# First loads in pieces with zero products, the query statistic moved into the attention steps, and twelve low parts moved from GpSimd to VectorE

## The chip, the core and the metric

The kernel runs on one core of one Trainium2 chip. The metric is the device time of one execution in microseconds. Engines are called TensorE (PE in the profile), VectorE (DVE), ScalarE (ACT), GpSimd (POOL) and SyncE (SP).

## What is computed

Four layers act on a stream of 272 tokens (16 meta tokens and 256 others) of width 1024, in fp32. Only what the change touches is shown; the rest is MLPs, a short convolution, a spatial gating mixer and convolutional feed-forward layers, all of them products with weight matrices of 1024 to 4096 rows.

```python
hn = rms_norm(h, g_mix[0])
z = hn @ w_in                                   # c_q, c_kv, k_pe, fox q, fox k, fox v, forget logit
q = (rms_norm(c_q, g_cq) @ w_uq).reshape(b, l, 8, 96)
q = rope_tail(rms_norm(q, g_q_mla), cos, sin)   # one statistic for each token and head
o_fox = blocked_causal_attention(qf, kf, vf, 64 ** -0.5, cum_log_f)   # 8 "fox" heads
o_mla = blocked_causal_attention(q, k, v_mla, 96 ** -0.5)             # 8 MLA heads
...
g, xb = jnp.split(h @ w_in, 2, axis=-1)         # recurrent mixer, width 1536
bterm = mult * (i * xb)
_, hs = lax.associative_scan(_lin_rec_op, (a, bterm), axis=1)
y = (hs * gelu(g)) @ w_out
```

## The kernel before

Activations lie feature-major: 128 features on the partitions, tokens along the free dimension. A weight matrix is cut into blocks of 128x128, and eight blocks (six in the down projections) make a unit. A product is done in three parts with both operands split into a high part (rounded) and a low part (the rest): high x high, high x low of the activation, low of the weight x high. So a unit of eight blocks is 24 matmuls on TensorE, into one PSUM bank. ScalarE makes the high part of each unit of weights (`split_hi`, L338), VectorE the low part (`split_lo`, L343), three units ahead (`LA = 3`), from slabs of two units (1024 KB) that SyncE loads into four places (`raw`). The same split is made of each activation: ScalarE makes `xhi` (L459), GpSimd `xlo` (L468), after VectorE has multiplied by the gain (`xg`, L449).

The order of the work is written out by hand for each engine; engines meet only at semaphores, and each runs its own list in order.

**The start.** ScalarE issues the load of the stream `h` (1088 KB), then the constants and selection rows; SyncE issues `params`, then the slabs. VectorE multiplies by the gain into two alternating buffers, so a third waits for GpSimd's low part of the first. TensorE waits for the constants, then does unit 0, waiting at each block for its `xlo`, then unit 1, then the column sum of `ssum` (`pe_stats`, L422), for which VectorE has added up eight squares (L1159). ScalarE takes the root (L435), VectorE the inverse (`rstd`, L442). Output tiles go round four PSUM banks: unit 4 starts when tile 0 has been read, which on VectorE needs `rstd` (L1231, L1232). Then come the forget gate (L1265 to L1278, on ScalarE L1590) and the statistic of the fox queries, whose inverse goes to TensorE at L852.

**The query statistic.** After the query projections (L956 to L958) TensorE does `q_stats` (L895): 42 small matmuls of 8 columns, in three groups. ScalarE takes the root (`roots(3)`, L1515, L1517), VectorE inverts and scales it (L1294 to L1304), and only then do the softmax steps begin, though the values are needed from item 9 on (the MLA heads). The attention goes over 18 items: item 0 and item 9 are small ones for the meta tokens, items 1 to 8 the fox heads, 10 to 17 the MLA heads. At step `st` TensorE does `scores(st)` (L995, L997), now and then a `spread` (L852), `turn(st - 2)`, the transposes of the probabilities (L1017, L1019), and `values(st - 3)` (L1033 to L1035); VectorE does the peak of the scores (L1313), the normalisation (L1332), a part of the keys up to step 7 (`k_normed`, L1200, L1204), and low parts (L1338); ScalarE the exponential (L1620) and copies.

**The recurrent mixer's end.** Steps `k` of a table (`B_SCAN`, `B_MULT`, `B_HIGH`) place the work. VectorE scans (L1470) and multiplies by the gate (L1475), ScalarE makes the high part (L1764), GpSimd the low part (L1947), for twelve tiles; TensorE's output projection `b_out` starts with two units of six blocks, which need the twelve tiles one after the other. Before it lies a dummy product (L1139).

## Time and profile before

| | |
|---|---|
| median of 3 runs | 1388.16 us (1387.38, 1388.16, 1391.67) |
| the profiled execution, time | 1393.52 us |
| the profiled execution, span | 1391.6 us |
| TensorE busy | 96% of the span |
| VectorE, ScalarE, GpSimd busy | 69%, 53%, 33% |

The span is the time from the first to the last instruction of the profiled execution; its time is 1.9 us longer. TensorE counts as busy while a matmul is in flight, also when the chip has granted it the lower of its two clocks, 1.2 GHz in place of 2.4 GHz; so the share of busy time does not tell of the clock.

### The profile page before, as it was taken

The page shows a single profiled execution, that of the slowest core. Times are in us where ns is not written, and L with a number is a line of the kernel's source. Part 1 is how long each engine was busy: PE and PEld are TensorE (multiplying, and loading weights), DVE is VectorE, ACT ScalarE, POOL GpSimd, SP SyncE. Part 2 cuts the span into 40 slices and gives each one's busy share as a digit, 9 for nine tenths or more (in the row PEclk, how much of TensorE's full clock was granted, in tenths as well). Part 3 has the DMA queues.
Part 4 walks back from the last instruction along what each step waited for, and adds up shares of the span by engine and source line. Part 5 has one row for each costly group of instructions (what it writes and reads, how often), then busy time and mean ns, then how long its engine had stood idle before and what let it go on. Part 6 is the DMA issues. An engine that isn't in the chain of part 4 may idle for free.

```text
span 1391.6 us, 29208 instructions
## 1 busy us (share of the span) xinstructions
PE 1334.9 (96%) x10776; PEld 1298.5 (93%) x10776; DVE 966.0 (69%) x1446; ACT 736.4 (53%) x1224; POOL 462.4 (33%) x492
## 2 busy tenths in 40 slices
PE   5999999999999999999999999999999969999997
PEld 5787699999999999999989999999998859999996
DVE  6767567664477677555655679997578786999844
ACT  5454645444444454444545456665446844766642
POOL 3532044321111443211636324333126563333310
PEclk9998999999999999999999999999999969999998
DMA  7440045555555555555525545554554426455451
GB/s 268 150 149 32 1 152 174 186 185 184 180 181 183 180 180 183 190 187 186 195 92 183 187 175 185 183 182 169 189 202 162 137 94 223 159 191 189 143 203 53
DMA packets 34508, 230.53 MB, mean 166 GB/s; under 512 B 3838, under 2 KB 4990, under 8 KB 10662
## 3 DMA queue, kind: packets, MB, share of 16 engines
q1 hardware_dynamic: 33652, 226.47, 46.8%
q10 hardware_dynamic: 770, 2.90, 0.6%
q8 instruction: 55, 0.90, 0.3%
q14 instruction: 31, 0.25, 0.1%
HBM read 228.17 MB, written 1.05 MB: 165 GB/s over the span
## 4 chain that ended last, share of the span: by engine, by line
PE 77%; issue 8%; DVE 6%; ACT 4%; POOL 4%; DMA 1%; POOLq 0%; DVEq 0%; ACTq 0%; SPq 0%
PE ps L378 25%; PE ps L379 25%; PE ps L380 25%; DVE wlo L343 2%; POOL xlo L468 2%; ACT whi L338 2%; POOL ssum L474 1%; PE ps L1085 1%; DMA raw<-w 1%; DVE rstd L442 1%; DVE work L1470 1%; POOL q_mla L1857 1%; DVE work L1441 0%; PE ps L422 0%; ACT work L1752 0%
## 5 line engine op out<-in xcount | busy, mean ns | idle before, releaser
L343 DVE TENSOR_TENSOR wlo<-raw,whi 128x1024 fp32r<-128x1024 f32 (+1 forms) x448 | 546.5, 1225 | 106.2 <-ACT whi L338 105.2
L378 PE MATMUL ps<-xhi,whi 128*128 128x256 f32 (+2 forms) x2064 | 586.5, 284 | 18.5 <-DVE wlo L343 13.9
L379 PE MATMUL ps<-xlo,whi 128*128 128x256 f32 (+2 forms) x2064 | 584.6, 283 | 0.0
L380 PE MATMUL ps<-xhi,wlo 128*128 128x256 f32 (+2 forms) x2064 | 583.5, 283 | 0.0
L338 ACT ACTIVATE whi<-raw 128x1024 fp32r<-128x1024 f32 (+1 forms) x448 | 448.5, 1008 | 141.2 <-PE ps L380 136.9
L378 PEld LDWEIGHTS ps<-xhi,whi 128*128 128x128 f32 x2064 | 391.9, 190 | 23.2 <-issue 15.9
L380 PEld LDWEIGHTS ps<-xhi,wlo 128*128 128x128 f32 x2064 | 392.3, 190 | 0.0
L379 PEld LDWEIGHTS ps<-xlo,whi 128*128 128x128 f32 x2064 | 389.9, 189 | 0.3
L378 PE MATMUL ps<-hhi,whi 128*128 128x256 f32 (+1 forms) x1184 | 338.0, 285 | 7.7 <-POOL hlo L1947 7.4
L380 PE MATMUL ps<-hhi,wlo 128*128 128x256 f32 (+1 forms) x1184 | 335.7, 283 | 0.0
L379 PE MATMUL ps<-hlo,whi 128*128 128x256 f32 (+1 forms) x1184 | 335.5, 283 | 0.0
L378 PEld LDWEIGHTS ps<-hhi,whi 128*128 128x128 f32 x1184 | 225.9, 191 | 10.6 <-POOL hlo L1947 4.9
L379 PEld LDWEIGHTS ps<-hlo,whi 128*128 128x128 f32 x1184 | 226.2, 191 | 0.0
L380 PEld LDWEIGHTS ps<-hhi,wlo 128*128 128x128 f32 x1184 | 226.1, 191 | 0.0
L468 POOL TENSOR_TENSOR xlo<-xg,xhi 128x256 f32 (+4 forms) x64 | 61.0, 954 | 354.8 <-ACT xhi L459 354.6
L647 POOL TENSOR_TENSOR work<-work 128x256 f32<-128x256 f32 x48 | 66.1, 1376 | 174.6 <-ACT work L603 169.1
L492 DVE TENSOR_TENSOR h<-ps,h 128x256 f32<-128x256 f32 (+3 forms) x64 | 27.2, 424 | 125.1 <-PE ps L380 125.1
L561 POOL TENSOR_TENSOR hlo<-act,hhi 128x258 f32 (+1 forms) x64 | 66.8, 1044 | 117.7 <-ACT hhi L553 117.7
L618 ACT ACTIVATE work<-tmp,params 128x256 f32<-128x256 f32 x96 | 57.7, 601 | 87.0 <-DVE tmp L588 87.0
L459 ACT ACTIVATE xhi<-xg 128x256 fp32r<-128x256 f32 (+4 forms) x64 | 26.6, 420 | 130.9 <-DVE xg L449 130.9
L553 ACT ACTIVATE hhi<-act 128x258 fp32r<-128x258 f32 (+3 forms) x64 | 26.9, 420 | 88.4 <-DVE act L540 88.4
L474 POOL TENSOR_TENSOR ssum<-ssum,sq 128x256 f32<-128x256 f32 (+1 forms) x64 | 45.9, 718 | 58.4 <-ACT sq L455 58.4
(262 smaller groups left out, 1314.3 us busy)
## 6 DMA issues: line engine op xcount, KB each, us to landing
raw<-w SPq DMA_DIRECT2D x184, 1024.0 KB, 4.9
raw<-w SPq DMA_DIRECT2D x40, 768.0 KB, 4.2
h<-x_fm ACTq DMA_DIRECT2D x1, 1088.0 KB, 6.4
out_fm<-h SPq DMA_DIRECT2D x8, 128.0 KB, 2.0
ws<-ws_src ACTq DMA_DIRECT2D x1, 512.0 KB, 5.0
bs<-bs_rows ACTq DMA_DIRECT2D x1, 512.0 KB, 5.8
consts<-constants ACTq DMA_DIRECT2D x1, 508.0 KB, 9.7
q_fox<-decay_rows SPq DMA_DIRECT2D x1, 340.0 KB
```

What stands on the lines that cost most here:

```text
L338: nc.scalar.activation(whi[:, j % HLR, 0:n], raw[:, slot, col:col + n], ACT.Copy).then_inc(whi_done, 1)
L343: nc.vector.tensor_tensor(wlo[:, j % HLR, 0:n], raw[:, slot, col:col + n], whi[:, j % HLR, 0:n].bitcast(F32), ALU.subtract).then_inc(wlo_d ...
L378: nc.tensor.matmul(o, hi, xh, start=start, stop=False)
L379: nc.tensor.matmul(o, hi, xl, start=False, stop=False)
L380: mm = nc.tensor.matmul(o, lo, xh, start=False, stop=stop)
L468: nc.gpsimd.tensor_tensor(xlo[:, kt, c0:c0 + t], xg[:, slot, 0:t], xhi[:, kt, c0:c0 + t].bitcast(F32), ALU.subtract).then_inc(xlo_done, 1)
L474: nc.gpsimd.tensor_tensor(ssum[:, c0:c0 + t], ssum[:, c0:c0 + t], sq[:, slot, 0:t], ALU.add).then_inc(ssum_done, 1)
L492: nc.vector.tensor_tensor(hh, ps[:, jt % ring + (4 - ring), 0:t], hh, ALU.add).then_inc(tile_free, 1)
L553: nc.scalar.activation(hi[:, k, 0:t], src[:, j % 2, 0:t], ACT.Copy).then_inc(uhi_done, 1)
L561: nc.gpsimd.tensor_tensor(lo[:, k, 0:t], src[:, j % 2, 0:t], hi[:, k, 0:t].bitcast(F32), ALU.subtract).then_inc(ulo_done, 1)
L618: nc.scalar.activation(cb[:, j % 4, :], tmp[:, j % 2, 0:SEQ], ACT.Identity, scale=par(f"f_conv_w{layer}", it * (3 * UB) + 3 * j + 2), bias ...
L647: nc.gpsimd.tensor_tensor(half[:, i % 2, :], gg[:, i % 2, :], cb[:, (2 * i + 1) % 4, :], ALU.mult).then_inc(u_done, 1)
```

## The change

Three parts. First, the start: `h` is loaded in four pieces with a semaphore each, `params` in two (the second one behind the slabs and the pad rows), the first slab in two halves; TensorE begins with 18 matmuls on a buffer that VectorE has set to zero, into a bank that is not otherwise in use; four gain buffers take the place of two; VectorE makes the low parts of the odd tiles, GpSimd those of the even ones; unit 0 and unit 1 do all high x high products first, then high x low, then low x high; the column sum goes behind unit 2, the sum of squares to GpSimd alone, and VectorE's inverse, with all that hangs on it, to the place of tile 3. Second, the three groups of `q_stats` go into `turn` of items 2, 3 and 4, into bank 6, `roots(3)` behind ScalarE's step 6, and VectorE's scaling into step 7. Third, the twelve low parts of the recurrent mixer go from GpSimd to VectorE, with a table `B_LOW` one step behind `B_HIGH`, and a step more in the loop.

```diff
-        x_loaded = sem("x_loaded")
+        x_loaded = [sem(f"x_loaded{i}") for i in range(4)]
+        xlo_odd = sem("xlo_odd")
...
-B_STEPS = max(*B_MULT, *B_HIGH, *B_GELU, 31) + 1
+B_LOW = steps(B_R5 + 10, (0, 1), (2, 3), (4, 5), (6, 7), (8, 9, 10, 11))
+B_STEPS = max(*B_LOW, *B_MULT, *B_HIGH, *B_GELU, 31) + 1
...
+        gained = [xg[:, 0, :], xg[:, 1, :], tmp[:, 0, :], tmp[:, 1, :]]
...
-            sp.dma_start(params[:, :], params_in).then_inc(small_in, 16)
+            first = pcol["conv_w"][0]
+            sp.dma_start(params[:, 0:first], params_in[:, 0:first]).then_inc(small_in, 16)
...
+                    half = UB * P
+                    sp.dma_start(raw[:, 0, 0:half], src[0][:, 0:half]).then_inc(s("unit0_loaded"), 16)
+                    sp.dma_start(raw[:, 0, half:cols], src[0][:, half:cols]).then_inc(raw_full[0], 16)
+                    for k in range(1, RAW):
+                        sp.dma_start(raw[:, k, 0:cols], src[k]).then_inc(raw_full[k], 16)
...
+                    rest = pcol["conv_w"][0]
+                    sp.dma_start(params[:, rest:npar], params_in[:, rest:npar]).then_inc(s("params_loaded"), 16)
...
-            pe.wait_ge(consts_in_done, 16)
+            pe.wait_ge(s("warm_set"), 1)
+            for _ in range(WARM):
+                nc.tensor.matmul(ps[:, 7, 0:SEQ], chi[:, 0, 0:P], chi[:, 0, 0:SEQ], start=True, stop=True)
...
+            def q_stats(k):
+
+                if k == 0:
+                    pe.wait_ge(q_eps_step, 6)
+                m = META if k == 2 else P
...
+                    mm = nc.tensor.matmul(ps[0:m, 6, 2 * P + k * HEADS:2 * P + (k + 1) * HEADS], lhs, rhs, start=x < 0,
+                                          stop=x == 5)
+                if k == 2:
+                    mm.then_inc(n_ss, 1)
...
+            def first_unit(u):
+
+                bank = take()
+                o = ps[:, bank, 0:T0]
+                pe.wait_ge(whi_done, u + 1)
+                for b in range(8):
+                    if u == 0:
+                        pe.wait_ge(xhi_done, b + 1)
+                    nc.tensor.matmul(o, whi[:, u, b * P:(b + 1) * P], xhi[:, b, :], start=b == 0, stop=False)
+                for b in range(8):
+                    if u == 0 and b % 2:
+                        pe.wait_ge(xlo_odd, (b + 1) // 2)
+                    elif u == 0:
+                        pe.wait_ge(xlo_done, b + 2)
+                    nc.tensor.matmul(o, whi[:, u, b * P:(b + 1) * P], xlo[:, b, :], start=False, stop=False)
+                pe.wait_ge(wlo_done, u + 1)
+                for b in range(8):
+                    mm = nc.tensor.matmul(o, wlo[:, u, b * P:(b + 1) * P], xhi[:, b, :], start=False, stop=b == 7)
+                mm.then_inc(unit_done, 1)
+
             for u in range(0, U_KN):
-                whole(u)
+                if u < 2:
+                    first_unit(u)
+                else:
+                    whole(u)
+                if u == 2:
+                    pe.wait_ge(consts_in_done, 16)
+                    pe_stats(pe, 0, 0, T0)
...
-            q_stats()
...
+                if j in (2, 3, 4):
+                    q_stats(j - 2)
+                if j == 5:
+                    pe.wait_ge(n_root, 4)
...
-                        pe.wait_ge(n_root, 4)
+                        pe.wait_ge(n_root, 3)
...
+            nc.vector.memset(chi[:, 0, :].bitcast(F32), 0.0).then_inc(s("warm_set"), 1)
             dve.wait_ge(small_in, 16)
-            dve.wait_ge(x_loaded, 16)
-            for kt in range(KT):
-                dve_gain(dve, 0, kt, kt % 2, 0, T0)
-                if kt == 4:
-                    split_lo(dve, 0, 0, 8)
-            for j in range(1, LA):
-                split_lo(dve, 0, j, 8)
-            for kt in range(KT):
-                dve.wait_ge(sq_done, kt + 1)
-                dve.wait_ge(ssum_done, kt + 1)
-                nc.vector.tensor_tensor(ssum[:, :], ssum[:, :], sq[:, kt % 2, :], ALU.add).then_inc(ssum_done, 1)
+
+            def first_gain(kt):
+                dve.wait_ge(x_loaded[kt // 2], 16)
+                if kt >= 4 and kt % 2 == 0:
+                    dve.wait_ge(xlo_done, kt - 2)
+                elif kt >= 4:
+                    dve.wait_ge(xlo_odd, (kt - 3) // 2)
+                nc.vector.tensor_scalar(gained[kt % 4], h[:, kt, :], par(NORM_GAIN[0], kt), None,
+                                        ALU.mult).then_inc(xg_done, 1)
+
+            def first_xlo(kt):
+                dve.wait_ge(xhi_done, kt + 1)
+                nc.vector.tensor_tensor(xlo[:, kt, :], gained[kt % 4], xhi[:, kt, :].bitcast(F32),
+                                        ALU.subtract).then_inc(xlo_odd, 1)
+            for kt in range(4):
+                first_gain(kt)
+            first_xlo(1)
+            first_gain(4)
+            first_gain(5)
+            first_xlo(3)
+            split_lo(dve, 0, 0, 8)
+            first_gain(6)
+            first_gain(7)
+            first_xlo(5)
+            split_lo(dve, 0, 1, 8)
+            first_xlo(7)
             nc.vector.memset(soft[:, :, :, :], 1.0).then_inc(s("soft_set"), 1)
             nc.vector.memset(q_inv[:, :, :], 1.0).then_inc(s("soft_set"), 2)
+            split_lo(dve, 0, 2, 8)
             split_lo(dve, 0, LA, 8)
-            dve_rstd(dve, 0, 0, T0)
...
-                if t == 0:
-
+                if t == 3:
+
+                    dve_rstd(dve, 0, 0, T0)
+                    dve.wait_ge(unit_done, 1)
+                    src = ps[:, 0, 0:T0]
...
-                if t == 1:
+                if t == 3:
...
+            def query_scale():
+                c = q_scale
+                dve.wait_ge(n_root, 4)
...
+                if st == 7:
+                    query_scale()
...
+                for t in B_LOW.get(k, ()):
+                    dve.wait_ge(uhi_done, hid0["b_in"] + t + 1)
+                    nc.vector.tensor_tensor(hlo2[:, t, :], xb[:, t, :], hhi2[:, t, :].bitcast(F32),
+                                            ALU.subtract).then_inc(ulo_done, 1)
...
-            act.dma_start(h[:, :, :], x_in).then_inc(x_loaded, 16)
+            for i in range(4):
+                act.dma_start(h[:, 2 * i:2 * i + 2, :], x_in[:, 2 * i:2 * i + 2, :]).then_inc(x_loaded[i], 16)
             act.dma_start(consts[:, :], consts_in).then_inc(consts_in_done, 16)
             act.dma_start(sel_in, rows_in).then_inc(rows_loaded, 16)
+
+            def first_xhi(kt):
+                act.wait_ge(xg_done, kt + 1)
+                nc.scalar.activation(xhi[:, kt, :], gained[kt % 4], ACT.Copy).then_inc(xhi_done, 1)
             for kt in range(KT):
-                act_xhi(act, 0, kt, kt % 2, 0, T0)
-                if kt in (2, 4, 6):
-                    split_hi(act, 0, kt // 2 - 1, 8, first=True)
+                first_xhi(kt)
+                if kt == 3:
+                    act.wait_ge(s("unit0_loaded"), 16)
+                    nc.scalar.activation(whi[:, 0, :], raw[:, 0, 0:UB * P], ACT.Copy).then_inc(whi_done, 1)
+                if kt in (5, 7):
+                    split_hi(act, 0, (kt - 3) // 2, 8, first=True)
             for kt in range(KT):
                 act_square(act, 0, kt, kt % 2, 0, T0)
-            split_hi(act, 0, LA, 8, first=True)
...
-            act_root(act, 0, 0, T0)
...
+                if t == 2:
+                    act_root(act, 0, 0, T0)
...
-            roots(3)
...
+                if st == 6:
+                    roots(3)
...
+            for kt in range(0, KT, 2):
+                pool.wait_ge(xhi_done, kt + 1)
+                nc.gpsimd.tensor_tensor(xlo[:, kt, :], gained[kt % 4], xhi[:, kt, :].bitcast(F32),
+                                        ALU.subtract).then_inc(xlo_done, 2)
             for kt in range(KT):
-                pool_xlo(pool, 0, kt, kt % 2, 0, T0)
+                pool_ssum(pool, 0, kt, kt % 2, 0, T0)
...
-            for t in range(NB):
-                pool.wait_ge(uhi_done, hid0["b_in"] + t + 1)
-                nc.gpsimd.tensor_tensor(hlo2[:, t, :], xb[:, t, :], hhi2[:, t, :].bitcast(F32),
-                                        ALU.subtract).then_inc(ulo_done, 1)
```

`B_LOW` puts tiles (0, 1) at `B_R5 + 10`, (2, 3) at + 11, (4, 5) at + 12, (6, 7) at + 13 and (8, 9, 10, 11) at + 14; `B_R5` is 21, `B_MULT` begins at + 7 and `B_HIGH` at + 9.

## Rows read from the trace of the kernel before

**Rows 1.** The page: busy time; then the longest waits of TensorE over the span.

```profile
PE 1334.9 (96%) x10776; PEld 1298.5 (93%) x10776; DVE 966.0 (69%) x1446; ACT 736.4 (53%) x1224; POOL 462.4 (33%) x492
...
PE ps L378 <- DVE wlo L343: 13.9, 4, 12.9
PE ps L378 <- POOL hlo L1947: 7.4, 5, 3.6
```

**Rows 2.** Timeline of the start: start us, us, engine line operation.

```profile
7.31 0.63 DVE L449 TENSOR_SCALAR xg<-h,params 128x272 f32<-128x272 f32 x2 [7.31 <-DMA h<-x_fm]
...
9.88 0.43 ACT L459 ACTIVATE xhi<-xg 128x272 fp32r<-128x272 f32 x1 [1.43 <-DVE xg L449]
10.39 0.76 POOL L468 TENSOR_TENSOR xlo<-xg,xhi 128x272 fp32r<-128x272 f32 x1 [0.70 <-ACT xhi L459]
10.47 1.06 ACT L338 ACTIVATE whi<-raw 128x1024 fp32r<-128x1024 f32 x1 [0.15 <-DMA raw<-w]
...
12.89 0.56 PE L378 MATMUL ps<-xhi,whi 128*128 128x272 f32 x1 [12.89 <-DVE wlo L343]
...
23.95 1.22 PE L422 MATMUL ps<-ssum,consts 128*128 128x272 f32 x2 [2.00 <-DVE ssum L1159]
...
24.23 1.28 ACT L435 ACT_TABLE_LOAD   x1
...
25.52 0.49 ACT L435 ACTIVATE root<-ps,params 128x272 f32<-128x272 f32 x1
...
26.04 1.85 DVE L442 RECIPROCAL rstd<-root 128x272 f32<-128x272 f32 x1 [0.57 <-ACT root L435]
```

**Rows 3.** DMA from 3 to 5 us: packets and MB of SyncE's queue (q1) and ScalarE's (q10).

```profile
q10 hardware_dynamic: 69, 0.60, 71.1%
q1 hardware_dynamic: 64, 0.16, 26.6%
```

**Rows 4.** Windows: stretch, length, busy (x instructions) of each engine, PEclk, DMA share, GB/s.

```profile
12.86:17.10 4.24, 4.21 (x18) 4.24 (x19) 2.59 (x4) 2.54 (x6) 2.84 (x5) 1.00 1.01 425
24.50:27.40 2.90, 2.90 (x13) 2.77 (x12) 2.33 (x2) 2.89 (x5) 0.39 (x1) 0.50 0.54 116
27.50:35.30 7.80, 7.80 (x64) 7.80 (x64) 6.97 (x10) 4.25 (x8) 0.00 (x0) 1.00 0.52 184
```

**Rows 5.** The chain that ended last: start us, us, what; unit 4's end, fox statistic.

```profile
35.35 0.03 ACT q_mla L1570
...
48.80 0.48 PE ps L852 x2
```

**Rows 6.** Timeline around the query statistic.

```profile
109.84 3.29 PE L895 MATMUL ps<-consts,early 128*128 128x8 f32 x28
109.89 0.90 DVE L1260 SCALAR_TENSOR_TENSOR early<-ps,params,consts 128x272 f32<-128x272 f32 x2
...
111.19 1.23 DVE L343 TENSOR_TENSOR wlo<-raw,whi 128x1024 fp32r<-128x1024 f32 x1 [0.40 <-ACT whi L338]
...
116.39 0.15 DVE L1313 TENSOR_REDUCE soft<-ps 16x1 f32<-16x16 f32 x1
```

**Rows 7.** Windows around the query statistic and over single attention steps.

```profile
109.84:113.46 3.62, 3.62 (x45) 3.60 (x44) 2.17 (x4) 1.06 (x1) 2.71 (x3) 0.91 0.79 253
...
120.81:124.28 3.47, 3.47 (x14) 3.08 (x14) 2.41 (x10) 0.99 (x5) 0.00 (x0) 0.50 0.00 0
128.91:132.17 3.26, 3.26 (x20) 2.26 (x19) 1.86 (x8) 1.50 (x7) 0.00 (x0) 1.00 0.02 5
```

**Rows 8.** VectorE's gate products (L1475): nanoseconds minimum, median, maximum.

```profile
L1475 DVE TENSOR_TENSOR work<-work x8: 393/411/950, 1125.5 to 1135.3; 128x256 f32<-128x256 f32 x8
```

**Rows 9.** Timeline of the recurrent mixer's end.

```profile
1127.36 2.53 DVE L1470 TENSOR_TENSOR_SCAN work<-work 128x256 f32<-128x256 f32 x3
1127.83 0.55 PE L378 MATMUL ps<-hhi,whi 128*128 128x256 f32 x1 [3.65 <-POOL hlo L1947]
...
1141.52 0.58 PE L378 MATMUL ps<-hhi,whi 128*128 128x256 f32 x1 [0.47 <-POOL hlo L1947]
...
1147.02 0.29 PE L379 MATMUL ps<-hlo,whi 128*128 128x256 f32 x1
```

More of the change, by code:

```diff
@@ L48 @@
 LA = 3
+WARM = 18
 PHASES = [
@@ L813, in whole @@
                 bank = take()
-                need = (lambda b: pe.wait_ge(xlo_done, b + 1)) if u == 0 else None
                 mm = unit(pe, u // UB, u % UB, [(ps[:, bank, 0:T0], b == 0, b == 7) for b in range(8)],
-                          [x_rhs(b, 0, T0) for b in range(8)], need)
+                          [x_rhs(b, 0, T0) for b in range(8)])
                 mm.then_inc(unit_done, 1)
-                if u == 1:
-                    pe_stats(pe, 0, 0, T0)
             ring = [0]
@@ L872, in k_stats @@
                 mm.then_inc(n_ss, 1)
-            def q_stats():
-                pe.wait_ge(n_root, 3)
-                pe.wait_ge(q_eps_step, 4)
-                for k in range(3):
-                    m = META if k == 2 else P
-                    for x in range(-1, 6):
-                        if k == 0 and x >= 0:
-                            pe.wait_ge(n_sq[3], x + 1)
-                        tile = q_eps if x < 0 else q_sq[:, x, :]
-                        if k == 2:
-                            pe.wait_ge(q_eps_step, 6)
-                            lhs = q_sq_d[:, META * (x + 1):META * (x + 2)]
-                        else:
-                            lhs = tile[:, NQ + k * P:NQ + (k + 1) * P]
-                        if x < 0:
-                            rhs = consts[:, K_LATENT:K_LATENT + HEADS]
-                        elif Q_KIND[x] == "nope":
-                            rhs = pair_cols(Q_AT[x])
-                        else:
-                            rhs = consts[:, K_QUAD + HEADS * Q_AT[x]:K_QUAD + HEADS * (Q_AT[x] + 1)]
-                        mm = nc.tensor.matmul(ps[0:m, 7, k * HEADS:(k + 1) * HEADS], lhs, rhs, start=x < 0, stop=x == 5)
-                mm.then_inc(n_ss, 1)
+            def q_stats(k):
+                if k == 0:
+                    pe.wait_ge(q_eps_step, 6)
+                m = META if k == 2 else P
+                for x in range(-1, 6):
+                    if k == 0 and x >= 0:
+                        pe.wait_ge(n_sq[3], x + 1)
+                    tile = q_eps if x < 0 else q_sq[:, x, :]
+                    if k == 2:
+                        lhs = q_sq_d[:, META * (x + 1):META * (x + 2)]
+                    else:
+                        lhs = tile[:, NQ + k * P:NQ + (k + 1) * P]
+                    if x < 0:
+                        rhs = consts[:, K_LATENT:K_LATENT + HEADS]
+                    elif Q_KIND[x] == "nope":
+                        rhs = pair_cols(Q_AT[x])
+                    else:
+                        rhs = consts[:, K_QUAD + HEADS * Q_AT[x]:K_QUAD + HEADS * (Q_AT[x] + 1)]
+                    mm = nc.tensor.matmul(ps[0:m, 6, 2 * P + k * HEADS:2 * P + (k + 1) * HEADS], lhs, rhs, start=x < 0,
+                                          stop=x == 5)
+                if k == 2:
+                    mm.then_inc(n_ss, 1)
             def turn_v(w):
```

35 lines of the change are left out of this document (18 added, 17 removed).

## The prediction

> **What bounds it now.** I read the page first: TensorE is in flight 96% of the span, and among its waits only a few places count: the first unit (12.9 us), and the low parts of the recurrent mixer (7.4 us) [rows 1]. A microsecond won where TensorE is late is kept, because from there on it has its list without long gaps. Then I read the start, the query statistic and the mixer's end in the timeline and the windows.
>
> At the start the stream is first touched at 7.3 us, the first slab at 10.5 us, and TensorE begins at 12.9 us [rows 2]. A unit of 24 matmuls costs 24 x 0.122 = 2.9 us at the high clock (64 in 7.80 us), and 24 x 0.223 = 5.4 us at the low one (13 in 2.90 us); the first 18 also went at 0.24 us each, so at the 1.2 GHz level, although the window's granted clock reads 1.00; there I go by the spacing [rows 4]. Unit 4 ended at 35.3 us, and from there a chain on ScalarE and VectorE ran to the spread at 48.8 us [rows 5]. I take 35.3 us as the milestone: what is won there is won in full, since that chain (13.5 us long) hangs on unit 4.
>
> **The start, worked out.** First the loads. From 3 to 5 us the two queues moved 69 and 64 packets, but 0.60 and 0.16 MB [rows 3]: they take turns by packets, not by bytes. Before, a packet of `h` was a partition's row of 8704 B; now a piece has rows of 2176 B, against 4096 B in half a slab and 8192 B in a whole one. With 0.42 MB/us in all [rows 4], and bytes flowing from about 2.6 us (7.3 us less the 2.0 MB that went till then), piece 0 (272 KB, beside 45 KB of parameters) is through at 3.4 us; piece 1 beside the first half slab (0.78 MB) at 5.3; piece 2 beside the second at 7.1; piece 3 beside a whole slab (1.3 MB) at 10.2. With 0.5 us to land: 3.9, 5.8, 7.6 and 10.7 us. So the last piece comes 3.4 us later than the whole of `h` does now.
>
> ScalarE makes four high parts (0.43 us each, the last after VectorE's gain of tile 3, at 7.0) and the first high weights (1.06) by 8.1 us [rows 2]: TensorE begins 4.8 us earlier. But it runs into tiles 6 and 7. From 10.7 us VectorE has in its list two gains (0.32 each [rows 2]), a low part (0.45, from 0.39 for 256 columns [rows 8]), unit 1's low weights (1.23 [rows 6]) and the low part of tile 7 (0.45): 13.5 us. GpSimd's low part of tile 6 (0.76 [rows 2]) may come in turn with one of them: 14.2 us. Then one matmul and eight of low x high at the low clock, 9 x 0.223 = 2.0: unit 0 ends at 16.3 us. TensorE works without a break from 12.2 us (high x low of the first tiles); before, such a stretch began at 12.9 and the spacing halved at 17.1 [rows 4], so I let it halve near 17: unit 1 ends at 16.3 + 3 x 0.223 + 21 x 0.122 = 19.6, unit 2 at 22.6 us. The sum of squares is hidden: eight additions of 0.76 from 13.4 us end by 20.5, under units 1 and 2; without that cover each 0.76 would be a delay.
>
> The 18 zero products have ended by 5 us (18 x 0.22 = 4.0 from about 0.8), under the loads, and cost nothing. I give them no gain either: 3 us without work follow.
>
> The stall goes on to unit 4, which needs tile 0 read. After unit 2: two reads of tile 2 on ScalarE (0.43 each), table load (1.28), root (0.49), inverse (1.85) [rows 2], two products of 0.45: 5.4 us, so 28.0 us. TensorE is through the column sum and unit 3 at 22.6 + 0.6 + 2.9 = 26.1. It waits 1.9 us; unit 4 ends at 28.0 + 2.9 = 30.9. **Start: 35.3 - 30.9 = -4.4 us.** Bounds: all pieces landed by 7.6 us and no wait at unit 4, -7; a rate of 0.35 MB/us with the high clock a unit later, -2.5. The second part of the parameters is waited for only after the attention, over 100 us later: nothing. The pad rows are where they were.
>
> **The query statistic.** The three groups and what is left of the scores' way fill 3.62 us [rows 7]. Without them the first peak follows VectorE's last evacuation and low weights (111.19 + 1.23 = 112.4 us) in place of 116.4: -3.9 us [rows 6]. In turns 2 to 4 they are on TensorE's path again: a step in the middle takes 3.26 us with TensorE in flight 3.26 [rows 7], so there is no gap to hide them: +3.6 at the high clock. ScalarE gets two table loads of 1.28 and two small roots at step 6, some 3 us, against 3.26 - 1.50 = 1.8 us of slack a step: 1.2 us late. VectorE's six small operations come in step 7, with the next peak queued behind; from the end of the products (113.5) to the peak (116.4) root and scaling took 2.9 us [rows 6, 7], of which I give VectorE 2.2. TensorE reads step j's exponentials two steps later, so I take 0.5 us of these. **Sum: -3.9 + 3.6 + 0.5 = +0.2 us.** This goes by the low clock in the first steps, as now (0.50) [rows 7]. If the clock stays high there, the first steps are bound by VectorE's 2.4 us a step [rows 7], the groups fall partly into waits, and it is -2.4; if the low clock lasts one step longer than now (3.3 us) and doubles one group (1.5), +5. I take the first, because the gaps between the first scores stay.
>
> **The low parts.** TensorE ends the 12 tiles' first blocks late: the last begins at 1141.5, and its clock is low until 1147.0 [rows 9]. Now VectorE has, from 1127.4: three scans (2.53), then in steps 29 to 35 twelve minus two products, two low weights of six blocks (0.75 x 1.23 = 0.95), and twelve low parts. A product takes 0.39 us at least, 0.95 at most, the long ones where GpSimd works [rows 8]; with GpSimd idle: 1129.9 + 10 x 0.39 + 2 x 0.95 + 12 x 0.39 = 1140.4 us for the last low part, of which the first comes at about 1134.2 in place of before 1127.8. TensorE, cold after a longer wait, needs 12 x 0.64 = 7.7 us: 1141.9, against 1141.5 + 0.64 = 1142.2. The tiles alone give 0.3. But after 1137 it has no gap; the clock rises that much earlier, at 1141 to 1144 in place of 1147.0, and half of the difference is won: 2.2. **Sum: -2.4 us.** Bounds: clock at 1140, -3.4; products and low parts at 0.7 us (halfway), 8 us more work less what is left of TensorE's slack, +3.
>
> A rule that speaks against this part: the Trainium skill, "Perfetto Trace Analysis", Optimizing Scalar/DVE Operations, says that VectorE and GpSimd share a read port, so that moving work from one to the other may not help. The rows show the shared cost (0.39 and 0.95 us), and it goes when one of the two is idle; by the rule taken strictly the part would give 0 and the time would be 1384.0 in place of 1381.6.
>
> **The sum.** -4.4 + 0.2 - 2.4 = -6.6 us (a little under 0.5%). The profiled execution, 1393.5 us (1391.6 of span and 1.9 around it), would be 1386.9. It lies 5.3 us over the median, and nothing in the three places says that they hold the difference; so the same is taken off the median: 1388.2 - 6.6 = 1381.6.
>
> **The rivals.**
> 1. *The clock stays high in the first attention steps.* For: the small products, during which it fell (0.91 in that window), are gone. Against: a gap of 1 us before the first scores remains. -2.4 in place of +0.2: 1379.0. Chance 0.18.
> 2. *The zero products keep TensorE fast until unit 0.* Nine and some 11 other matmuls at 0.122: -2.1, so 1379.5. Against: the 2.0 us without work before the column sum were followed by a clock of 0.50 [rows 2, 4]. Chance 0.10. The Trainium skill, "TensorE: Matmul & The Clock Gate", Part 1, has sustained activity raise the clock and idleness lower it; what it makes of 3 us of idleness no row here shows.
> 3. *VectorE's low parts don't pay* (contention was not the cause of 0.95, or order delays the first ones): 0 to +3, 1384 to 1387. For: VectorE is in flight all of this time already. Chance 0.14.
> 4. *Slower: the groups hold the clock low through steps 4 to 6.* Three steps at 6.5 in place of 3.26 (+9.8) and the groups twice (+3.6): +13.4 against the forecast, so 1395. It decides from two steps on: one costs 3.3, which the other parts pay for. For: during these products the clock fell. Against: 4 us of other matmuls between two groups. Chance 0.05.
> 5. *The query part costs 3 to 5 us* by one slow step: 1385 to 1387. Chance 0.08.
> The forecast itself: 0.45, from 1379 to 1384.
>
> A measurement of this kernel tells some 0.3% (4.2 us) from no change. Below 1384.0 lie the forecast, rivals 1 and 2 and a little of 3: 0.77; above 1392.3 rival 4: 0.05; the rest 0.18. Range 1376.5 to 1387: the forecast with either bound of the start, rivals 1, 2, 3 and 5.
>
> **What would show it.** Right: TensorE's first unit begins near 8 us, with gaps before tiles 6 and 7; piece 3 lands after 10 us; unit 0 ends near 16; a wait of 1.9 us before unit 4; unit 4 ends near 31. The first peak near 112.4 less 4.4; no gap around the small products, whose 28 wide ones still take 3.3 us. At the mixer's end products and low parts of 0.4 us, TensorE beginning 6 us later and without gap after. Wrong: a low clock through the middle steps, an exponential more than 2 us late at step 7, products of 0.9 us with GpSimd idle, or piece 3 at 7 us.

## The result and the profile after

The changed kernel took 1396.13 us (median of 20 runs, 1389.28 to 1406.69), the kernel before 1388.78 us (20 runs beside them, 1384.97 to 1393.82). The ratio is 1.0057, 95% interval 1.0042 to 1.0072: slower by 0.6%, where the forecast was 1381.6 us and gave a slower kernel 0.05. The times of before lie within 9 us, those of the changed kernel within 17.4. Of all executions reported here one was slow as a whole, one of e1's twelve with 1462.28 us at a mean granted clock of 0.84; it is left out of the ratio.

The page of the changed kernel, busy time and TensorE's longest waits (as [rows 1]; us in total, times, longest):

```profile
PE 1341.3 (96%) x10794; PEld 1302.6 (93%) x10794; DVE 962.3 (69%) x1455; ACT 739.0 (53%) x1226; POOL 457.5 (33%) x484
...
PE ps L381 <- DVE hlo L1541: 9.2, 1, 9.2
PE ps L381 <- DVE extra L1291: 4.6, 1, 4.6
...
PE ps L927 <- ACT whi L1568: 3.8, 1, 3.8
...
PE ps L862 <- DVE k_mla L1260: 3.4, 2, 1.9
```

TensorE's busy time has hardly changed, which says little: a matmul at half the clock is busy too. What is new is a wait of 4.6 us for tile 0 (`extra`), one of 3.8 ahead of the first unit, and two for `k_mla` (the keys of the MLA heads, which VectorE normalises between its softmax steps). The span grew by 9.1 us (1391.6 to 1400.7). This profile is of one execution, which took 1402.43 us, 6.3 above the median.

**The start** (timeline of the changed kernel; answers to [rows 2]):

```profile
1.27 4.21 PE L814 MATMUL ps<-chi 128*128 128x256 f32 x18 [1.27 <-DVE chi L1188]
...
4.00 0.63 DVE L1197 TENSOR_SCALAR xg<-h,params 128x272 f32<-128x272 f32 x2 [2.78 <-DMA h<-x_fm]
...
9.30 1.73 PE L927 MATMUL ps<-xhi,whi 128*128 128x272 f32 x6 [3.81 <-ACT whi L1568]
...
12.38 0.63 DVE L1197 TENSOR_SCALAR tmp<-h,params 128x272 f32<-128x272 f32 x2 [1.02 <-DMA h<-x_fm]
...
15.44 8.96 POOL L477 TENSOR_TENSOR ssum<-ssum,sq 128x272 f32<-128x272 f32 x8
...
17.96 1.64 PE L927 MATMUL ps<-xhi,whi 128*128 128x272 f32 x8
...
27.38 0.49 ACT L438 ACTIVATE root<-ps,params 128x272 f32<-128x272 f32 x1
...
28.85 1.23 DVE L346 TENSOR_TENSOR wlo<-raw,whi 128x1024 fp32r<-128x1024 f32 x1 [1.82 <-ACT whi L341]
29.99 1.85 DVE L445 RECIPROCAL rstd<-root 128x272 f32<-128x272 f32 x1
...
32.83 0.59 PE L381 MATMUL ps<-xhi,whi 128*128 128x272 f32 x1 [4.56 <-DVE extra L1291]
```

The reader is to see that TensorE starts its first unit 3.6 us earlier (9.30 against 12.89) and has nothing of it at unit 4: the last piece of `h` is worked on at 12.38, unit 1 begins at 17.96, and unit 4 at 32.83, after a wait, and at the low clock (the window from 32.83 to 37.6 us has a granted clock of 0.66). Unit 4 ends at 37.6 in place of 35.3 us.

**The attention** (TensorE's timeline around the query products, then windows as in [rows 7], changed kernel):

```profile
124.46 0.39 PE L862 MATMUL ps<-inv,sel 40*128 40x272 f32 x1 [1.55 <-DVE k_mla L1260]
124.78 3.14 PE L903 MATMUL ps<-consts,early 128*128 128x8 f32 x14
...
133.84 2.99 PE L903 MATMUL ps<-consts,early 128*128 128x8 f32 x14
...
143.42 0.54 PE L903 MATMUL ps<-consts,extra 128*16 128x8 f32 x14
```

```profile
120.00:124.00 4.00, 2.73 (x19) 2.17 (x17) 3.80 (x12) 2.05 (x11) 1.30 (x3) 1.00 0.00 0
...
128.00:132.00 4.00, 4.00 (x13) 2.19 (x12) 0.00 (x0) 1.21 (x4) 0.00 (x0) 0.50 0.00 0
...
148.00:152.00 4.00, 4.00 (x15) 2.75 (x14) 1.67 (x7) 2.23 (x7) 0.00 (x0) 0.50 0.00 0
152.00:156.00 4.00, 4.00 (x15) 2.84 (x15) 2.15 (x9) 1.15 (x5) 0.00 (x0) 0.56 0.01 4
```

Before, the clock was at half from about 113 to 126 us and then high. Here it is high through the first scores, falls at 124.8, behind two waits for `k_mla` and as the first group begins, and stays at half to 155.3 us: 30 us. From the first scores to the last values the heads took 61.0 us before (114.66 to 175.62), 77.1 now (114.04 to 191.09).

**The mixer's end** (timeline, VectorE's products and low parts in ns, windows; answers to [rows 8, 9]):

```profile
1147.04 0.55 PE L381 MATMUL ps<-hhi,whi 128*128 128x256 f32 x1 [9.22 <-DVE hlo L1541]
```

```profile
L1538 DVE TENSOR_TENSOR work<-work x8: 393/414/416, 1139.1 to 1146.1; 128x256 f32<-128x256 f32 x8
...
L1541 DVE TENSOR_TENSOR hlo<-work,hhi x12: 414/418/422, 1146.5 to 1151.5; 128x256 fp32r<-128x256 f32 x12
```

```profile
1147.04:1152.20 5.16, 5.16 (x24) 5.16 (x25) 5.16 (x16) 3.16 (x6) 0.00 (x0) 0.50 0.14 58
...
1152.00:1154.00 2.00, 2.00 (x18) 2.00 (x17) 0.90 (x2) 0.17 (x1) 0.00 (x0) 0.94 0.11 15
```

One wait of 9.2 us in place of several, then no gap, and the clock up at 1152.2. Measured from the small product that stands ahead of these matmuls in both kernels (1123.63 before, 1137.27 now), the clock rises after 14.9 us in place of 23.4. No product takes 0.95 us any more.

### The profile page after: what moved, and what is told of

It is laid out like the page before. It is cut to its first block, busy times and chain, and to the rows that moved or that the text cites. A ratio compares the mean times of both kernels' runs of the same rounds, so it can differ in the third digit from the quotient of the medians.

```text
span 1400.7 us, 29261 instructions
## 1 busy us (share of the span) xinstructions
PE 1341.3 (96%) x10794; PEld 1302.6 (93%) x10794; DVE 962.3 (69%) x1455; ACT 739.0 (53%) x1226; POOL 457.5 (33%) x484
## 4 chain that ended last, share of the span: by engine, by line
PE 76%; issue 9%; DVE 6%; ACT 4%; POOL 4%; DMA 1%; ACTq 0%; POOLq 0%; DVEq 0%
PE ps L381 25%; PE ps L383 24%; PE ps L382 24%; DVE wlo L346 2%; POOL xlo L471 2%; ACT whi L341 2%; POOL ssum L477 1%; DVE rstd L445 1%; DMA h<-x_fm 1%; PE ps L1125 1%; DVE work L1533 1%; POOL q_mla L1939 1%; DVE work L1504 0%; ACT work L1830 0%; PE ps L844 0%
## 5 line engine op out<-in xcount | busy, mean ns | idle before, releaser
L341 ACT ACTIVATE whi<-raw 128x1024 fp32r<-128x1024 f32 (+2 forms) x447 | 447.4, 1008 | 140.6 <-PE ps L383 136.7
L471 POOL TENSOR_TENSOR xlo<-xg,xhi 128x256 f32 (+3 forms) x56 | 53.8, 961 | 373.3 <-ACT xhi L462 373.1
L462 ACT ACTIVATE xhi<-xg 128x256 fp32r<-128x256 f32 (+3 forms) x56 | 23.5, 420 | 123.0 <-DVE xg L452 123.0
L477 POOL TENSOR_TENSOR ssum<-ssum,sq 128x256 f32<-128x256 f32 (+2 forms) x72 | 54.0, 750 | 59.4 <-ACT sq L458 58.4
```

The lines of the kernel that those rows point to most:

```text
L341: nc.scalar.activation(whi[:, j % HLR, 0:n], raw[:, slot, col:col + n], ACT.Copy).then_inc(whi_done, 1)
L471: nc.gpsimd.tensor_tensor(xlo[:, kt, c0:c0 + t], xg[:, slot, 0:t], xhi[:, kt, c0:c0 + t].bitcast(F32), ALU.subtract).then_inc(xlo_done, 1)
L477: nc.gpsimd.tensor_tensor(ssum[:, c0:c0 + t], ssum[:, c0:c0 + t], sq[:, slot, 0:t], ALU.add).then_inc(ssum_done, 1)
```

## The experiments

All were timed in five rounds beside the kernel before, twelve times each where no other number is given. The ratio with its 95% interval is not the quotient of the two medians, but within 0.001 of it (e7: 0.9978 and 0.9968). The kernel before has medians from 1387.82 to 1389.60 us in the different rounds, so kernels of different rounds are compared by their ratios.

**The parts alone.** Their edits are the hunks of the change's own diff. e1 has those of the start (loads, first units, zero products, sum of squares, VectorE's order), e2 those of the query statistic, e3 those of the mixer's low parts, and e4 is e1 and e3 together. Of e2 and e3 the core:

```diff
-            q_stats()
...
+                if j in (2, 3, 4):
+                    q_stats(j - 2)
+                if j == 5:
+                    pe.wait_ge(n_root, 4)
```

```diff
+B_LOW = steps(B_R5 + 10, (0, 1), (2, 3), (4, 5), (6, 7), (8, 9, 10, 11))
+B_STEPS = max(*B_LOW, *B_MULT, *B_HIGH, *B_GELU, 31) + 1
```

> The kernel before with the start part alone (loads in pieces, zero products, new order of units 0 and 1, inverse at tile 3). Theory (the inverse lies behind unit 6's low weights in VectorE's list, and these behind ScalarE's root): unit 4 begins late, as in the changed kernel's trace (4.6 us of waiting), the clock is low after it, and the part costs about 2 us: ratio 1.001 to 1.003. Rival (the prediction's): it gains 4.4 us and the whole loss lies elsewhere: ratio 0.997.

Measured: 1391.45 us, 1.0022 (1.0007 to 1.0036). The start costs some 3 us (1 to 5). TensorE's wait before unit 4 is again 4.56 us.

> The kernel before with the query part alone (the three groups of small products inside turns 2 to 4, root at step 6, scaling at step 7). Theory (the small products come where TensorE's clock has fallen, and it stays low through steps 4 to 8): 8 to 13 us slower in most executions, and executions that scatter by 10 us, ratio about 1.007. Rival (only the added table loads and scaling cost): 0 to 2 us, ratio 1.000 to 1.0015, with no more scatter than before.

Measured: 1395.62 us, 1.0060 (1.0035 to 1.0084), from 1389.08 to 1406.43. This part carries the loss, and the scatter. The mean granted clock was 0.985 in its shortest run and 0.973 in its longest; 0.012 of some 1400 us is 34 us more at half the clock, and as work goes at half the speed there, half of that, 17 us, is what they cost. The two runs differ by 17.4. So the clock explains most of the scatter (three runs at 0.981 still lie 4.5 us apart). Of the loss it explains a part. The means are 0.9804 for e2's runs and 0.9840 for the 35 of the kernel before: by the same estimate 5 us, an upper value, as not all work waits for TensorE. Some 3 us of the 8.3 are left for the groups' own time and for waits.

> The kernel before with the twelve low parts on VectorE alone. Theory (no turn-taking of VectorE and GpSimd, and an earlier high clock in the output projection): 3 to 4.5 us faster, ratio 0.997. Rival (the difference in the two traces came from the clock alone, by chance): 0 to 1 us.

Measured: 1386.78 us, 0.9987 (0.9972 to 1.0002): 1.8 us off, not separated from nothing by itself.

> The changed kernel with the query part taken back. Theory: the parts add up, +2 for the start and -4 for the low parts, so about 2 us faster than before, ratio 0.9985, with no scatter beyond that of before. Rival (the start part by itself makes the attention slow, as its shift against the clock's own rhythm puts the low clock there): as slow as the changed kernel, ratio 1.005.

Measured: 1388.61 us, 1.0000 (0.9985 to 1.0015). By their ratios the parts add up within what the intervals allow: +3.1, +8.3 and -1.8 make +9.6, the whole measured +7.9 (5.8 to 10.0).

**What of the query part costs.** e5 leaves the products and roots ahead of the scores, and moves VectorE's scaling alone; e6 puts the groups two turns later, the roots two steps and the scaling one.

Against the query part alone, e5 and then e6:

```diff
-                if j in (2, 3, 4):
-                    q_stats(j - 2)
...
+            for k in range(3):
+                q_stats(k)
```

```diff
-                if j in (2, 3, 4):
-                    q_stats(j - 2)
+                if j in (4, 5, 6):
+                    q_stats(j - 4)
```

> The query part with its products left where the kernel before has them: the 21 products of the three groups and the roots stand ahead of the scores and the exponentials, and only VectorE's scaling moves to step 7 of the heads. No product is added to the attention's first steps. Theory (the products inside the steps hold TensorE's clock low): without them the loss of some 8 us goes, the twelve times scatter no more than those of before (4 us instead of 17), and VectorE's scaling off the way gives 1 to 3 us: 1385 to 1388. Rival (the late scaling and what waits for it are the loss): as the query part alone, 1392 to 1398 with the same scatter.

Measured: 1389.55 us, 1.0000 (0.9986 to 1.0014), 1386.34 to 1391.43. The loss and the scatter are gone, and the late scaling is not the cause (the late root stands in e9). The gain of 1 to 3 us that I expected of it isn't there either.

> The query part with its three groups of small products two turns later, in turns 4, 5 and 6, the roots and the scaling at step 8. Theory (what hurts is that the groups come while the clock is still low, and keep it there): in turns 4 to 6 the profile of before has the clock high, each group costs what it measured at the high clock (0.5 us) or little more, and the loss falls from 8 us to 1 to 3: 1388 to 1392, with less scatter. Rival (a group drops the clock wherever it stands): as the query part alone, 1393 to 1398, and the granted clock falls to one half after one of the groups in the profile.

Measured: 1397.27 us, 1.0060 (1.0041 to 1.0079; six runs), 1395.68 to 1398.92. The size follows the rival, and the range of the theory is missed. But the mean clock of its runs, 0.9810 against 0.9829 of the kernel before, makes only 2.6 us of the 8.1 by the estimate above; more of the loss is the groups' own time and waits, so e6 doesn't show that the place leaves the clock as it was. Its trace shows one sequence in the open, at a clock that was high (TensorE's timeline, then windows):

```profile
129.59 1.73 PE L893 MATMUL ps<-consts,early 128*128 128x8 f32 x14
...
136.06 1.63 PE L893 MATMUL ps<-consts,early 128*128 128x8 f32 x14
...
145.53 0.38 PE L1020 MATMUL ps<-consts,wide 128*16 128x128 f32 x2 [1.49 <-ACT q_inv L1523]
```

```profile
131.00:132.00 1.00, 1.00 (x9) 0.81 (x10) 0.94 (x3) 0.29 (x3) 0.00 (x0) 1.00 0.00 0
132.00:133.00 1.00, 1.00 (x4) 0.42 (x3) 0.23 (x1) 0.76 (x3) 0.00 (x0) 0.80 0.03 8
...
135.00:136.00 1.00, 1.00 (x4) 0.76 (x4) 0.00 (x0) 0.00 (x0) 0.00 (x0) 0.50 0.00 0
136.00:137.00 1.00, 1.00 (x12) 1.00 (x10) 0.71 (x3) 0.00 (x0) 0.00 (x0) 0.99 0.00 0
```

The group runs at the high clock; behind it, with TensorE busy all the time, the clock is at half until 136. The second group is not followed by that, so a group doesn't bring the low clock each time. And TensorE waits 1.49 us for the late root and 0.82 behind that, with a second stretch at half from 146.6 to 153 us.

**The products themselves.** e9 takes most of them out (it leaves out the statistic of the first two groups, which is a constant there), e11 and e12 add one group to the kernel before, of 8 and of 128 columns. e9 against the query part, then e11 against the kernel before (e12 has `P` for `HEADS` and reads the constants from `K_ONES`):

```diff
+                if k < 2:
+                    if k == 0:
+                        pe.wait_ge(n_sq[3], 6)
+                    nc.tensor.matmul(ps[:, 6, 2 * P + k * HEADS:2 * P + (k + 1) * HEADS], ones, ones[:, 0:HEADS],
+                                     start=True, stop=True)
+                    return
```

```diff
+                if j == 4:
+                    for x in range(7):
+                        lhs = (q_eps if x == 6 else q_sq[:, x, :])[:, NQ:NQ + P]
+                        nc.tensor.matmul(ps[:, 6, 2 * P:2 * P + HEADS], lhs, consts[:, K_PAIR:K_PAIR + HEADS], start=x == 0,
+                                         stop=x == 6)
```

> The query part alone, but the first two groups compute nothing: each is one product of two constant matrices in place of seven products of the squares, so the query statistic of the queries' first two blocks is a constant. The third group, the roots in the exponentials' turn, the scaling on VectorE and all waits stay. Theory (the small products are the loss, by their own time and by the low clock that they hold): the 8 us go, and 1 to 3 us are gained on the kernel before, 1385 to 1388, with times that scatter over 6 us or less. Rival (the root's change of table, the wait for it at turn 5 and the scaling at step 7 are the loss): 1393 to 1397.

Measured: 1388.09 us, 1.0002 (0.9991 to 1.0013), 1385.49 to 1390.32. The loss and the scatter go with the products. Nothing is gained on the kernel before: 2.9 us are won ahead of the scores (from TensorE's wait for `v_tok` to the first scores 8.1 us, 101.93 to 110.06, in place of 11.0, 103.68 to 114.66), and then TensorE waits for VectorE and for the root:

```profile
115.39 0.59 PE L852 MATMUL ps<-inv,sel 40*128 40x272 f32 x1 [2.24 <-DVE k_mla L1211]
...
133.68 0.38 PE L1024 MATMUL ps<-consts,wide 128*16 128x128 f32 x2 [0.45 <-ACT q_inv L1527]
```

Its clock fell too, with no group near: the first of the constant products comes at 122.04. Windows of e9:

```profile
113.00:115.00 2.00, 0.15 (x2) 0.00 (x0) 1.90 (x5) 0.94 (x4) 1.71 (x3) 0.92 0.01 4
115.00:121.00 6.00, 5.61 (x21) 4.83 (x22) 5.28 (x17) 2.37 (x12) 2.39 (x5) 0.50 0.00 0
```

TensorE had next to nothing to do from 113 to 115 us, and the clock was at half from 115 to 121. In the changed kernel two such waits stand ahead of 124.8. So the fall there is not shown to be the groups' doing; what they add, by these two traces, is its length, 30 us in place of some 7.

> The kernel before with one more group of seven products of the squares with 8 columns of constants, in turn 4 of the heads, where the clock of before is high; nobody reads what they write. Theory (such a group costs its own 1.7 us and is followed by some 4 us at half the clock, which cost 2 more): 2.5 to 4.5 us slower, 1391 to 1393, and the profile shows a granted clock of 0.50 within 3 us behind the group. Rival (a group costs its own time alone): 1.5 to 2 us slower and the clock stays at 1.00.

> The same, with 128 columns in place of 8 in each of the seven products. Theory (the 8-column products leave TensorE with little work for its time, and that lowers the clock): the seven take 2.5 to 3.5 us, more than those of 8 columns, but no low clock follows them; 2.5 to 3.5 us slower than the kernel before. Rival (whatever stands between the heads' products delays VectorE and ScalarE, and that brings the low clock): a low clock as behind the narrow group, and 4.5 us or more slower.

Measured: narrow 1390.39 us, 1.0022 (1.0011 to 1.0033); wide 1390.83 us, 1.0024 (1.0013 to 1.0036). The group's matmuls and weight loads in ns, and the windows behind it, of the narrow one and then of the wide one:

```profile
L1012 PEld LDWEIGHTS ps<-consts,early x14: 186/192/192, 131.9 to 133.4; 128*128 128x128 f32 x14
L1012 PE MATMUL ps<-consts,early x14: 256/256/277, 131.9 to 133.4; 128*128 128x8 f32 x14
```

```profile
132.00:135.00 3.00, 3.00 (x23) 2.35 (x24) 2.41 (x9) 1.70 (x7) 0.00 (x0) 1.00 0.01 3
135.00:138.00 3.00, 3.00 (x11) 2.23 (x10) 0.00 (x0) 0.45 (x2) 0.00 (x0) 0.50 0.00 0
```

```profile
L1012 PE MATMUL ps<-consts,early x14: 275/275/377, 132.1 to 133.7; 128*128 128x128 f32 x14
```

```profile
132.00:135.00 3.00, 3.00 (x22) 2.28 (x21) 2.64 (x9) 1.40 (x7) 0.00 (x0) 1.00 0.01 3
135.00:138.00 3.00, 3.00 (x20) 2.26 (x19) 0.70 (x3) 0.77 (x3) 0.00 (x0) 1.00 0.00 0
```

In the traces the difference is plain: behind 8 columns the clock is at half from 135 us, and 11 matmuls run in 3 us where 20 do behind 128 columns. And 128 columns take hardly longer (14 in 1.83 us against 1.73, not the 2.5 to 3.5 that I expected). In the medians the two are the same, and so is the mean clock of their twelve runs (0.9832 and 0.9829): the difference is shown by one trace of each, no more. What the low clock costs here is 1.6 us (the first MLA item begins 30.9 us after the first scores with the narrow group and 29.4 with the wide one, whose own time is 0.1 longer), near to what these intervals can tell apart.

**The same products, wider, in the changed kernel.** Each of the 21 writes its 8 columns 16 times over; a later group overwrites only columns that nobody reads.

```diff
-                    mm = nc.tensor.matmul(ps[0:m, 6, 2 * P + k * HEADS:2 * P + (k + 1) * HEADS], lhs, rhs, start=x < 0,
-                                          stop=x == 5)
+                    o = ps[0:m, 6, 2 * P + k * HEADS:3 * P + k * HEADS].rearrange("p (r h) -> p r h", h=HEADS)
+                    rhs = rhs.rearrange("p (r h) -> p r h", h=HEADS).broadcast_to([P, P // HEADS, HEADS])
+                    mm = nc.tensor.matmul(o, lhs, rhs, start=x < 0, stop=x == 5)
```

> The query part alone, with each of its 21 products writing its 8 columns 16 times over, 128 columns in all; the sums that are read are the same. Theory (narrow products keep the clock low): the clock rises at about 123 us and stays high, the products cost their own 4 us or, at the low clock, up to 6 us; 1388 to 1391, with times that scatter over 6 us or less in place of 17. Rival (in the first steps any added product, wide or narrow, keeps the clock low): as with 8 columns, 1394 to 1397, with the same scatter.

> The changed kernel whole, with the same widening. Theory: the part of the loss that is the clock goes, and what stays is the sum of the start (+3), the low parts (-2) and the wide products (+1 to +3): 1388 to 1392, against 1396 with narrow ones. Rival (the groups' place, not their width): 1394 to 1398.

Measured: query part 1392.70 us, 1.0023 (1.0010 to 1.0035), 1389.24 to 1395.26; whole change 1392.27 us, 1.0026 (1.0014 to 1.0039), 1390.02 to 1394.00, in place of 1396.13 and 17 us of scatter. The query part came out 1.7 us over its range, between theory and rival, but with the small scatter. Here the clocks of all runs bear the theory out: 0.9850 in the mean for the query part, where the narrow one had 0.9804 and the kernel before 0.9838, and 0.9828 for the whole change, where the narrow one had 0.9795. The 3.2 us that the wide query part still costs are then not the clock: in its profile the three groups take 5.3 us, and TensorE waits 2.2 us for `k_mla`. Windows of the whole change with wide products:

```profile
125.00:130.00 5.00, 3.44 (x17) 3.10 (x16) 3.82 (x13) 2.59 (x11) 0.00 (x0) 0.72 0.01 3
130.00:135.00 5.00, 5.00 (x33) 3.95 (x32) 1.15 (x6) 1.53 (x6) 0.00 (x0) 0.94 0.00 0
135.00:140.00 5.00, 5.00 (x34) 3.60 (x34) 2.99 (x11) 2.33 (x11) 0.00 (x0) 1.00 0.00 2
```

The clock fell at 127.2 us, again behind waits for `k_mla` and at the first group, and is up again by 131, in place of 155. With more columns to compute the kernel is about 4 us faster.

**The start.** e7 is the change without its query part (e4), with the reciprocal and the two products of tile 0 ahead of `to(tile_unit[t])`. e8 is e7 with `h` in one transfer. e10 is e8 with `WARM = 0`.

```diff
             for t in range(N_TL):
+                if t == 3:
+                    dve_rstd(dve, 0, 0, T0)
...
                 to(tile_unit[t])
...
-            for i in range(4):
-                act.dma_start(h[:, 2 * i:2 * i + 2, :], x_in[:, 2 * i:2 * i + 2, :]).then_inc(x_loaded[i], 16)
+            act.dma_start(h[:, :, :], x_in).then_inc(x_loaded[0], 16)
```

> The changed kernel without its query part, and with the reciprocal of tile 0's root and its two products of tile 0 on VectorE ahead of the low weights of unit 6. Theory (TensorE's wait of 4.6 us before unit 4 is set by the low weights that stand in front of the reciprocal): the reciprocal begins right behind the root, about 27.9 instead of 30.0, unit 4 begins 2.1 us sooner, and the time is about 2 us below that of the same kernel with the old order: 1386 to 1387. Rival (unit 6's low weights are then late by as much and TensorE waits there): no difference, 1388 to 1389, with a wait of 1 us or more ahead of unit 6's lo products.

Measured: 1385.10 us, 0.9978 (0.9965 to 0.9992). By the ratios that is 3.1 us below e4, where 2 were expected. VectorE and TensorE in its timeline:

```profile
27.68 1.85 DVE L445 RECIPROCAL rstd<-root 128x272 f32<-128x272 f32 x1 [0.86 <-ACT root L438]
...
30.50 1.23 DVE L346 TENSOR_TENSOR wlo<-raw,whi 128x1024 fp32r<-128x1024 f32 x1
...
30.53 0.39 PE L381 MATMUL ps<-xhi,whi 128*128 128x272 f32 x1 [2.48 <-DVE extra L1266]
```

The wait falls from 4.6 to 2.5 us, and unit 6's low weights come in time.

> The same kernel with h loaded in one transfer instead of four. Theory (the pieces land late, the last at 12.4 us, and VectorE's low parts of unit 0 follow them): in one transfer h lands as it did before the change, at about 9 us, VectorE's gains begin later but are done sooner, and unit 0 ends up to 1 us earlier or not at all; the time differs from the kernel in four pieces by less than 1 us. Rival (the pieces are worth what the change hoped): 1 to 2 us slower than in four pieces.

Measured: 1384.55 us, 0.9968 (0.9954 to 0.9982). VectorE has the whole of `h` at 7.17 us, where the last of four pieces came at 12.38; unit 1 begins at 17.89, against 17.59. By the ratios one load is 1.4 us faster, which the intervals don't separate from nothing. The pieces bring nothing that can be measured.

> The kernel with h in one transfer, the reciprocal first and GpSimd's low parts on VectorE, without the 18 products of zeros. Theory (the zero products bring nothing: TensorE waits 5.7 us after them until the first unit's weights are split, and its clock falls all the same): the same time within 1 us, 1384 to 1386. Rival (they keep the clock from falling in unit 0): without them unit 0 runs 2 us longer and the time is 1386 to 1388.

Measured: 1385.28 us, 0.9980 (0.9968 to 0.9993). By the ratios it is 1.7 us slower than e8, which the intervals (0.9954 to 0.9982 for e8) don't separate from nothing. The traces decide on the mechanism: the first six matmuls of unit 0 take 1.70 us without the zero products and 1.73 behind them (e8), some 0.29 each, so they go at the low clock's spacing in both. Unit 0 begins at 10.54 and unit 1 at 17.42, not later than with them.

e7 and e8 are faster than the kernel before and than the changed one.

## Why the prediction was wrong

Two steps failed, and each missed by about 8 us: the query part was forecast at +0.2 us and costs +8.3 (e2), the start at -4.4 and costs +3.1 (e1).

**The step that failed in the query part** is "+3.6 at the high clock", with "this goes by the low clock in the first steps, as now". It took the three groups to cost their own time and to leave the clock where it was. Each costs its own time (the first two took 3.4 us in the profile of e2, mostly at the high clock, 6.1 in the changed kernel), and with them the low clock lasts: 30 us at half. That is rival 4, which had a chance of 0.05. That its 1395 lies near 1396.13 is luck: it has the start's -4.4 in it, and 13.6 us for the query part, which costs 8.3. I had the row for it: during just these products before, the granted clock went to 0.91 [rows 7]; I read it as a sign for rival 1, that the gap and the products together lower the clock, and gave the matmuls between the groups as the reason against rival 4. The runs show that those matmuls don't make up for the groups (e2, and e13 and e14, where the same groups are wide and the loss shrinks). Rival 1 also happened, in part: the clock was high through the first scores. It bought nothing: TensorE then waited 3.4 us for VectorE's `k_mla`, and the groups followed.

**Its first term**, -3.9 us for the products taken from ahead of the scores (its rows give 116.39 - 112.42 = 4.0), measured -2.9 up to the first scores (e9). Of that nothing is left at the end: e9, which has the gain and hardly any group, is as slow as the kernel before (1.0002), as TensorE waits 2.2 us for `k_mla` (1.1 in e2, 3.4 in the changed kernel). That wait is in no term of the forecast. Moving VectorE's scaling is worth nothing that can be measured (e5). So, as an estimate, the query part's +8.3 is some 3 us for the groups with nothing won ahead of them, and up to 5 for the clock. The -2.4 that was given to a high clock in the first steps has no working.

**The start**, -4.4 forecast, measured +3.1. Unit 4 ended at 37.6 in place of the 30.9 that I had worked out. The pieces landed in the order foreseen, the first on time and the others 1.4, 1.6 and 1.7 us late (the 0.5 us to land that the forecast allows is in no row); unit 2 ended at 24.5 in place of 22.6. "The sum of squares is hidden" came true with nothing to spare: GpSimd's eight additions took 1.12 us in the mean (0.77 to 1.75), not 0.76, and ended at 24.4, just ahead of the column sum at 24.54, which did not wait; in e4 and e7, whose unit 2 ended earlier, it waited 0.5 us. The root ended at 27.9 in place of 25.2. Then comes an error of order, 2.1 us: I let the inverse follow the root, and it stood behind `to(3)`, so behind the low weights of unit 6, which wait for ScalarE's high ones at 27.8 to 28.8. Tile 0 was read at 32.8, not 28.0. Then unit 4 ran mostly at the low clock, 4.8 us in place of 2.9 (granted clock 0.66 in that window), which the step "unit 4 ends at 28.0 + 2.9" left out although it had the wait in it. e7 mends the order alone and gives back some 3 us; its unit 4 ends at 35.4, where it ended before. So the early start of TensorE was never worth what I gave it: the chain of sum, root and inverse sets unit 4, and nothing of the change makes that chain shorter.

**The zero products** bring nothing, as foreseen, and nothing that they cost was measured; rival 2 is refuted by the spacing of unit 0's matmuls (e8, e10). **The loads in pieces**: e8 shows no gain.

**The low parts** went as worked out, only better (the forecast's 0.3 and 2.2 make 2.5, not 2.4): products of 0.39 to 0.42 us without exception, last low part at 1151.9, which is 14.6 us after the small product, where I had 16.8. In the profiled execution the part is worth 4.5 us (the changed kernel lay 13.6 us behind before the mixer's end, 9.1 at the end of the span), in the medians 1.8 alone, which its interval doesn't separate from nothing, and 2.8 as the difference of e4 and e1; the forecast was 2.4. The rule of the Trainium skill, "Perfetto Trace Analysis", Optimizing Scalar/DVE Operations, that moving work between VectorE and GpSimd might not help, doesn't decide here: the shared cost goes once GpSimd is idle. At the start the same sharing is seen in full: GpSimd's low part of tile 4, beside VectorE's low weights, took 1.76 us, the first one 0.76.

What stays open: 9 of the 20 runs of the changed kernel took 1389.3 to 1392.4 us and 11 took 1395.8 to 1406.7. The clock goes with it, 0.980 to 0.985 in the nine and 0.971 to 0.981 in the eleven; what decides after which group it rises again was not found. That e14 stays 3.6 us over the kernel before is the sum of the start (+3.1), the low parts (-1.8 to -2.8) and the wide products (+3.2 in e13), but of e13's 3.2 us the groups' own time and the wait for `k_mla` were not parted. And no run fills the waits for `k_mla`, so how much of the low clock comes from them is open.

## What to carry to other kernels

Before work is put between other work on TensorE, ask what it does to the clock and not only how long it takes: with three groups of 8 columns the mean granted clock fell from 0.984 to 0.980, with the same groups at 128 columns it did not (0.985), though they took 1.4 us longer (5.3 in place of 3.9). Work that is taken away ahead of a stage wins only what the next wait leaves of it: 2.9 us were won and none kept. When a chain (sum, root, inverse) sets a milestone, an earlier start of the engine that waits for it is worth nothing; and where an operation moves to a new place in an engine's list, read what stands in front of it there and what that waits for. Test the parts of a combined change apart: here one part seems to have paid and two cost, and the repaired combination of two was the fastest kernel.

## What was not expected of the hardware

The width of the products. Fourteen fp32 matmuls of 8 columns took 1.73 us and of 128 columns 1.83, one each 0.12 to 0.13 us, as with the 272 columns of a unit (64 in 7.80 us). Each has a weight load of its own, of 0.19 us, that overlaps its neighbours; that these loads set the pace is not shown. All through, the profile shows TensorE as busy (3.00 of 3.00 us) while its clock falls to 0.50. The Trainium skill, "TensorE: Matmul & The Clock Gate", Part 1, ties the clock to how busy the engine has been; by the traces of e11 and e12, one of each, that is not the busy time of the profile, since both have the same and only one loses the clock. The runs of e13 against e2 point the same way.

The pieces of `h`: in four transfers of 272 KB beside the slabs the last quarter was there at 12.5 us (e7), in one transfer the whole at 7.2 (e8, which differs in that alone). Splitting a load that runs beside larger ones made its end 5 us later.
